# A two-layer hybrid backbone: the scan stage's decays in other buffers and first in a group, masks ahead of scaled keys, recurrence steps dealt out anew, gates loaded apart from rows

## The chip, the cores and the metric

The kernel runs on one core of one Trainium2 chip. The metric is the device time of one execution in microseconds; the figure given is the median of three runs. A profiled execution has a trace beside its own time.

## The reference, cut to what matters

Two layers are applied to 128 prompt rows and to 1024 sample rows. A layer projects its input, runs three token mixers on the same projection, projects their outputs together, and then applies a mixture of 16 experts. The change is in the token mixers: latent attention with 4 heads, gated linear attention (GLA) with 4 heads, and a gated delta net (GDN) with 8 heads. The last two run over chunks of 64 rows, in both directions. For the delta net a chunk needs the inverse of a unit lower triangular 64x64 matrix, and a state that goes from chunk to chunk:

```python
def gdn_chunked(q, k, v, beta, log_a, s0):
    ...
    g = jnp.cumsum(log_a, axis=2)
    ...
    m = jnp.einsum('bnihk,bnjhk->bnhij', k_beta, k) * jnp.exp(jnp.where(strict, diff, -jnp.inf))
    t_inv = lax.linalg.triangular_solve(m, eye, left_side=True, lower=True, unit_diagonal=True)
    u = jnp.einsum('bnhij,bnjhv->bnihv', t_inv, v * beta[..., None])
    w = jnp.einsum('bnhij,bnjhk->bnihk', t_inv, k_beta * jnp.exp(g)[..., None])
    qk = jnp.einsum('bnihk,bnjhk->bnhij', q, k) * jnp.exp(jnp.where(incl, diff, -jnp.inf))
    ...
    def step(s, inp):
        qc, kc, uc, wc, ac, dl = inp
        v_new = uc - jnp.einsum('bihk,bhkv->bihv', wc, s)
        o = jnp.einsum('bihk,bhkv->bihv', qc, s) + jnp.einsum('bhij,bjhv->bihv', ac, v_new)
        s = s * jnp.exp(dl)[..., None, None] + jnp.einsum('bihk,bihv->bhkv', kc, v_new)
        return s, o
```

## The kernel before

Each layer is a row of stages with barriers between them: `front` (projection), `scan` (the three mixers), `mixer_output`, `experts`. Each engine runs its own list of instructions in the order in which the code writes them; waits between engines are semaphores, counted from 1. The change touches `scan` alone.

`scan` (L939) goes through five groups of chunks (2, 4, 4, 4 and 4 chunks of 64 rows). Both directions are worked at once, one in partitions 0 to 63, the other in 64 to 127. A group g does this for the delta net:

- **Head.** `small` (cumulated gates, TensorE, then an exponential `eg` on ScalarE); `turn_keys` and `turn_queries` (TensorE transposes, evicted by ScalarE to `kq`); `decays` (two matmuls of 128x512 for each half of the group, then the exponential `dec` on ScalarE); on GpSimd `scaled_keys` (eight operations) and `mask` (four, on `dec`); `grams` (TensorE) and `masked_grams` (VectorE, grams times `dec`).
- **Solve.** `block_in` and `block_scaled` (VectorE) bring the diagonal 32x32 blocks to `NB` and `Tb`, in the buffer `late`; `substitute` (GpSimd, L1812) inverts them in 30 dependent steps of two operations, between the semaphores `sub_in` and `sub_done`.
- **Tail.** VectorE turns the six solved blocks back: `inverse_for_x` (two, signals `nb_v`), `inverse(1)` and `inverse(2)` (signal `ta_v`), `inverse(0)` and `inverse(3)` (`tb_v`). TensorE joins the blocks by `merge_x` (waits for `nb_v` and for `sg_v`), `merge_z` (waits for `ta_v`), then `weights` (waits for `tb_v`) and `values`; ScalarE evicts each.
- **Recurrence.** The chunks of the group k = g - 1 go through `read_state` (TensorE reads the state, VectorE corrects the values) and `write_state` (TensorE, then VectorE adds), in the course of group g.

The rest of a group is filled with GLA, two halves of two chunks each (`gla_gates`, `gla_turn`, `gla_scores`, `gla_values`, then `gla_state` twice; VectorE signals `sg_v` at the end of each `gla_state`), and with units of latent attention (`attend(i)`): odd units are scores, even ones turn the probabilities. Which step stands between which is written out by hand, for each engine by itself. SP issues the loads and stores in an order of its own, each wait holding up what follows. After group 4 the four chunks of its recurrence run in a last stretch with the last attention units, while SP loads for the next stage (`load_next`).

`dec` lies in the first half of `early`, whose second half holds the keys; E holds the gates of GLA, `gin` its rows.

## Time and profile before

| | us |
|---|---|
| median of 3 runs (4412.68 to 4423.40) | 4415.18 |
| profiled execution, its own time | 4419.75 |
| its span in the trace | 4418.0 |
| TensorE busy | 3911.6 (89%) |
| VectorE, ScalarE, GpSimd busy | 2156.0, 971.5, 1050.0 |
| scan of layer 0 (from its first matmul, 578.2, to the next stage's, 1141.3) | 563.1 |
| scan of layer 1 (2761.8 to 3322.3) | 560.5 |

A stage's length is not read from the shares of the whole span, which mix stages with different limits. Within the scan a group lasts from the end of one `values` to the end of the next. Busy time of TensorE is that of pipelined matmuls with modelled ends. Times in a timeline are counted from the span's start.

### The profile page before, as it was taken

What the parts mean: (1) busy time and instruction counts of PE and PEld (TensorE: products, weight loads), DVE (VectorE), ACT (ScalarE), POOL (GpSimd) and SP (SyncE); (2) the same over time, 40 slices, a digit from 0 to 9 for tenths busy, and PEclk for the clock granted to TensorE, in tenths of its full rate; (3) what the DMA queues carried; (4) which work ended last, traced back from release to release, by engine and by line L of the source; (5) the groups of instructions that cost most, each with busy time, mean ns of one, the idle gap of its engine ahead of it and who ended that gap; (6) DMA issues with size and microseconds to landing.
All of it is one profiled execution on the core that took longest, in us unless ns stands there. A gap on an engine that the chain in (4) does not pass through costs nothing. (4 is left out here: it accounts for less than half of the span.)

```text
span 4418.0 us, 80607 instructions
## 1 busy us (share of the span) xinstructions
PE 3911.6 (89%) x33780; PEld 3014.1 (68%) x33780; DVE 2156.0 (49%) x4908; ACT 971.5 (22%) x1962; POOL 1050.0 (24%) x1088
## 2 busy tenths in 40 slices
PE   4999968788897999999869998788888799999995
PEld 3444446676556999999844445466764489999995
DVE  3335045665555444544453440556656564445445
ACT  1233134444210000000033331444441100000001
POOL 0036035454220100001040360345432100011002
PEclk9999978888998999999989999888889899999998
DMA  7557353331526888888564651533325278888886
GB/s 262 175 186 247 137 132 68 89 72 52 195 86 209 292 279 284 282 290 293 176 229 162 220 206 56 126 78 81 73 84 204 81 236 285 287 293 280 287 289 208
DMA packets 557880, 836.20 MB, mean 189 GB/s; under 512 B 85865, under 2 KB 403369, under 8 KB 551373
## 3 DMA queue, kind: packets, MB, share of 16 engines
q1 hardware_dynamic: 474476, 720.51, 50.1%
q10 hardware_dynamic: 67840, 71.59, 4.9%
q0 software_dynamic: 15200, 38.94, 3.5%
q8 instruction: 267, 4.37, 0.4%
q14 instruction: 97, 0.79, 0.1%
HBM read 698.83 MB, written 132.10 MB: 188 GB/s over the span
## 5 line engine op out<-in xcount | busy, mean ns | idle before, releaser
L2611 PE MATMUL ffn_hb<-ffn_xT,ffn_w 128*128 128x144 f32 x8192 | 1048.5, 286 | 0.0
L2611 PEld LDWEIGHTS ffn_hb<-ffn_xT,ffn_w 128*128 128x128 f32 x8192 | 1019.6, 190 | 2.3 <-issue 1.0
L521 PE MATMUL front_acc<-late,front_xmT 128*128 128x512 f32 (+2 forms) x2304 | 879.7, 541 | 21.6 <-DVE front_xmT L782 18.3
L521 PEld LDWEIGHTS front_acc<-late,front_xmT 128*128 128x128 f32 x2304 | 437.3, 192 | 450.0 <-issue 419.0
L2619 PE MATMUL ffn_acc<-ffn_hT,ffn_w 128*128 128x144 f32 x4096 | 547.2, 287 | 0.0
L2619 PEld LDWEIGHTS ffn_acc<-ffn_hT,ffn_w 128*128 128x128 f32 x4096 | 518.5, 190 | 6.7 <-issue 6.7
L2654 ACT ACTIVATE ffn_en<-ffn_hb 128x144 f32<-128x144 f32 x256 | 74.2, 290 | 1447.0 <-PE ffn_hb L2611 1447.0
L2534 POOL DMA_INDIRECT ffn_xe<-scratch_xhat,ffn_g_idx x34 | 34.2, 1005 | 1478.0 <-DVEq L2719 1435.9
L2763 DVE TENSOR_TENSOR ffn_hT<-ffn_en,ffn_hb 128x144 f32<-128x144 f32 x256 | 77.8, 304 | 582.3 <-ACT ffn_en L2654 581.9
L2287 PE MATMUL mixer_acc<-late,mixer_oT 128*128 128x512 f32 x576 | 250.7, 593 | 3.0 <-ACT mixer_oT L2253 3.0
L2680 DVE TENSOR_SCALAR_CACHE_REDUCE ffn_junk<-ffn_row,ffn_pair 128x128 f32<-128x128 f32 (+2 forms) x324 | 245.3, 757 | 1.5
L1817 POOL TENSOR_TENSOR scan_prod<-late 128x30 f32<-128x30 f32 (+5 forms) x300 | 182.6, 609 | 221.7 <-POOLq L1834 199.0
L591 POOL TENSOR_TENSOR x_res<-x_res,early 128x1536 f32<-128x1536 f32 x18 | 72.4, 4022 | 554.1 <-DMA x_res<-scratch_proj 554.1
L2287 PEld LDWEIGHTS mixer_acc<-late,mixer_oT 128*128 128x128 f32 x576 | 108.0, 190 | 133.0 <-issue 129.1
L2679 DVE TENSOR_SCALAR_CACHE_REDUCE ffn_junk<-ffn_row,ffn_pair 128x128 f32<-128x128 f32 (+6 forms) x252 | 187.2, 743 | 4.4
L1370 PE MATMUL scan_ring<-x_res 128*128 128x512 f32 (+1 forms) x400 | 160.4, 534 | 12.2 <-ACT x_res L1674 4.5
L1819 POOL TENSOR_TENSOR late<-late,scan_prod 128x30 f32<-128x30 f32 (+5 forms) x300 | 162.6, 542 | 23.5
L1981 DVE TENSOR_REDUCE scan_top<-x_res 128x1 f32<-128x1152 f32 (+1 forms) x72 | 88.7, 1232 | 145.0 <-ACT x_res L1678 126.6
L1351 PE MATMUL scan_ring<-x_res 128*128 128x64 f32 x1168 | 138.9, 272 | 0.9 <-ACT x_res L1701 0.9
L1351 PEld LDWEIGHTS scan_ring<-x_res 128*128 128x128 f32 x1168 | 136.6, 192 | 1.4 <-ACT x_res L1701 1.2
L649 ACT ACTIVATE front_out<-front_acc 128x512 f32<-128x512 f32 (+1 forms) x90 | 49.7, 552 | 392.7 <-PE front_acc L521 392.7
L1370 PEld LDWEIGHTS scan_ring<-x_res 128*128 128x128 f32 x400 | 68.9, 199 | 97.2 <-ACT x_res L1674 48.2
(349 smaller groups left out, 5190.3 us busy)
## 6 DMA issues: line engine op xcount, KB each, us to landing
ffn_w<-in_w_e SPq DMA_DIRECT2D x384, 1024.0 KB, 9.4
x_res<-in_w_mod SPq DMA_DIRECT2D x40, 1024.0 KB, 5.7
x_res<-scratch_proj SPq DMA_DIRECT2D x36, 768.0 KB, 6.3
scratch_proj<-front_out ACTq DMA_DIRECT2D x90, 256.0 KB, 2.2
ffn_row<-scratch_affT SPq DMA_DIRECT2D x36, 576.0 KB, 4.5
late<-in_w_in ACTq DMA_DIRECT2D x8, 2048.0 KB, 12.1
early<-scratch_qkv SPq DMA_DIRECT2D x16, 1024.0 KB, 10.2
scratch_qkv<-x_res SPq DMA_DIRECT2D x18, 768.0 KB, 3.5
```

Of the source, the lines that this page charges most:

```text
L521: mm = pe.matmul(acc[:, U % 2, 0:size], xmT[:, k, t * P:(t + 1) * P], w[:, n % 2, k, 0:size], start=k == 0, stop=k == KD - 1)
L1351: mm = pe.matmul(b[:, P:P + VD], probT[:, k * P:(k + 1) * P], kv[:, h % 2, KEYS_W + (j0 + k) * VD:KEYS_W + (j0 + k + 1) * VD], start=k == ...
L1370: mm = pe.matmul(ring[:, i % 2, 0:size], qT[:, n % 4, :], kv[:, h % 2, k0 + at:k0 + at + size], start=True, stop=True)
L1817: pool.tensor_tensor(x, wide(Tb[:, 0:i, i], n), NB[:, i + 1:32, i].unsqueeze(1).to_broadcast([P, i, n]), ALU.mult).then_inc(own, step())
L1819: pool.tensor_tensor(Tb[:, 0:i, i + 1:32], Tb[:, 0:i, i + 1:32], x, ALU.add).then_inc(own, step())
L1981: dve.tensor_reduce(top[:, c], prob[:, n % 2, 0:w], AX.X, ALU.max).then_inc(own, step())
L2287: mm = pe.matmul(acc[:, t % 2, n * 512:(n + 1) * 512], oT[:, t % 2, k, :], wout[:, k, n * 512:(n + 1) * 512], start=k == 0, stop=k == KD - 1)
L2611: mm = pe.matmul(hb[:, b, i * CAP:(i + 1) * CAP], w[:, r, k, c:c + P], xT[:, s, k, :], start=k == 0, stop=k == KD - 1)
L2619: mm = pe.matmul(part(c), w2[:, r, j % WIDTH, c * P:(c + 1) * P], hT[:, b, :], start=j == 0 and c % PER_BANK == 0, stop=j == KF - 1, skip_ ...
L2679: dve.tensor_scalar(junk[:, 0:a - lo], row[:, lo:a], mine, 0.0, ALU.is_ge, ALU.add, accum_out=counts[:, t, 0:1]).then_inc(own, step())
L2680: dve.tensor_scalar(junk[:, a - lo:hi - lo], row[:, a:hi], mine, 0.0, ALU.is_gt, ALU.add, accum_out=counts[:, t, 1:2]).then_inc(own, step())
L2763: dve.tensor_tensor(hT[:, b, :], en[:, b], hb[:, b, CAP:2 * CAP], ALU.mult).then_inc(h_done, 1)
```

## The change

On every engine that takes part, the order within a group is written anew. The decays come first in a group from group 1 on, ahead of `small`, and are put where the solve's `NB` and `Tb` lie, so they wait for the group before to be turned. GpSimd masks before it scales keys. The recurrence of a group of four chunks had two chunks in the head and two in the filling; now the head has the last chunk's write of the group before it and chunk 0, the filling has chunks 1 and 2, and the last chunk's read stands between `merge_x` and `merge_z`. VectorE does both `gla_state` of the second half ahead of turning the blocks. TensorE gets two matmuls more, whose result nobody reads, between `sub_done` and `merge_x`. SP loads the gates (E) apart from the rows, and earlier. Lines of after are numbered by up to 32 more than those of before.

```diff
-dec = qk[:, :, 0:DQ]
+dec = B.late[:, 6 * 1024:8 * 1024].rearrange("p (m c) -> p m c", m=4)
...
+def load_gla_gates(h):
+    if h > 0:
+        sp.wait_ge(gT_p, h + 1)
+    for d in range(2):
+        sp.dma_start(E[half(d)], rows("gla_la", d, h * P, P, d * GQ, (d + 1) * GQ)).then_inc(ge_in, 16)
+
 def load_gla(h):
     if h > 0:
         sp.wait_ge(gV_p, h + 1)
     for d in range(2):
         sp.dma_start(gin[half(d)], rows("proj", d, h * P, P, C_GQ, C_GLR)).then_inc(gl_in, 16)
-        sp.dma_start(E[half(d)], rows("gla_la", d, h * P, P, d * GQ, (d + 1) * GQ)).then_inc(gl_in, 16)
...
     g = k + 1
     if g == GROUPS:
         load_next()
-    if k >= 0:
-        for m in range(2):
+    if g == GROUPS:
+        store_gdn(k - 1, 3)
+        for m in range(4):
             store_gdn(k, m)
-    if g < GROUPS:
-        if k >= 0 and g + 1 < GROUPS:
-            load_gates(g + 1)
-        if g + 1 < GROUPS:
-            load_qk(g + 1)
-        h = halves[g][0]
-        if h < 8:
-            load_gla(h + 1)
+        break
     if k >= 1:
-        for m in range(2, 4):
-            store_gdn(k, m)
-    if k >= 0 and k + 2 < GROUPS:
-        load_v(k + 2)
-    if k == 0:
+        store_gdn(k - 1, chunks[k - 1] - 1)
+        load_v(g)
+    if k == 1:
         sp.wait_ge(s_v, 3)
         for d in range(2):
             for a in range(2):
...
-    if g < GROUPS:
-        for h in halves[g]:
-            if h != halves[g][0] and h < 8:
-                load_gla(h + 1)
-            store_gla(h)
+    if k >= 0:
+        store_gdn(k, 0)
+        if g + 1 < GROUPS:
+            load_gates(g + 1)
+    if g + 1 < GROUPS:
+        load_qk(g + 1)
+    if halves[g][0] < 8:
+        load_gla_gates(halves[g][0] + 1)
+    if k >= 1:
+        store_gdn(k, 1)
+    if halves[g][0] < 8:
+        load_gla(halves[g][0] + 1)
+    if k >= 1:
+        store_gdn(k, 2)
+    for h in halves[g]:
+        if h != halves[g][0] and h < 8:
+            load_gla_gates(h + 1)
+            load_gla(h + 1)
+        store_gla(h)
...
 def turn_keys(g, i):
-    h = halves[g][i]
     if i == 0:
         pe.wait_ge(qk_in, 32 * g + 33)
-        if g:
-            pe.wait_ge(w_a, h + 1)
-    else:
-        pe.wait_ge(eg_a, g + 2)
+    if g:
+        pe.wait_ge(E_a, halves[g][i] + 2)
...
 def decays(g, i):
     pe.wait_ge(laM_l, g + 2)
-    pe.wait_ge(qT_a, halves[g][i] + 2)
+    if g == 0:
+        pe.wait_ge(qT_a, halves[g][i] + 2)
+    elif i == 0:
+        pe.wait_ge(w_a, halves[g][0] + 1)
+    else:
+        pe.wait_ge(eg_a, g + 2)
...
 def grams(g, m):
     s = g % 2
     if m < 2:
-        pe.wait_ge(E_a, halves[g][min(m, len(halves[g]) - 1)] + 2)
+        i = min(m, len(halves[g]) - 1)
+        pe.wait_ge(qT_a, halves[g][i] + 2)
+        pe.wait_ge(E_a, halves[g][i] + 2)
         pe.wait_ge(eg_a, g + 2)
...
     if g == GROUPS:
+        write_state(k - 1, 3)
         for m in range(4):
...
     else:
+        decays(g, 0)
+        small(g)
+        if k:
+            write_state(k - 1, chunks[k - 1] - 1)
+        decays(g, 1)
         for i in range(n):
             turn_keys(g, i)
         read_state(k, 0)
         for i in range(n):
             turn_queries(g, i)
-        write_state(k, 0)
-        for i in range(n):
-            decays(g, i)
-        read_state(k, 1)
         for m in range(2):
             grams(g, m)
-        write_state(k, 1)
+        write_state(k, 0)
         for m in range(2, chunks[g]):
             grams(g, m)
         attend(at)
...
         attend(at + 7)
         gla_state(g, h, 1)
         h = halves[g][1]
+        gla_gates(g, h)
         attend(at + 8)
-        gla_gates(g, h)
+        gla_turn(g, h)
         attend(at + 9)
-        gla_turn(g, h)
+        gla_scores(g, h)
         attend(at + 10)
-        gla_scores(g, h)
+        gla_values(g, h)
         attend(at + 11)
-        gla_values(g, h)
+        gla_state(g, h, 0)
         attend(at + 12)
-        gla_state(g, h, 0)
-        attend(at + 13)
         gla_state(g, h, 1)
-        attend(at + 14)
+        for i in range(13, 15):
+            attend(at + i)
     if g > 1:
         gla_gates(g, h)
         attend(at + 1)
...
         gla_turn(g, h)
-        write_state(k, 2)
+        write_state(k, 1)
         gla_scores(g, h)
         attend(at + 3)
         gla_values(g, h)
-        read_state(k, 3)
+        read_state(k, 2)
...
         attend(at + 9)
         gla_state(g, h, 0)
+        gla_state(g, h, 1)
         attend(at + 10)
-        gla_state(g, h, 1)
         attend(at + 11)
+    if g:
+        pe.wait_ge(o_v, first[k] + chunks[k])
+        pe.wait_ge(sub_done, g + 2)
+        for _ in range(2):
+            pe.matmul(pR[:, 0, :], ident, B.masks[:].rearrange("p k c -> p (k c)"), start=True, stop=True)
     for i in range(n):
         merge_x(g, i)
+    if g:
+        read_state(k, chunks[k] - 1)
     for i in range(n):
         merge_z(g, i)
...
 def decays(g, i):
     act.wait_ge(D_p, halves[g][i] + 2)
+    if g:
+        act.wait_ge(ta_v, 2 * g + 1)
+        act.wait_ge(tb_v, 2 * g + 1)
     act.activation(dec[:, 2 * i:2 * i + 2, :], pA[:, 2 * i:2 * i + 2, :], ACT.Exp).then_inc(E_a, 1)
...
+        decays(g, 0)
+        small(g)
+        decays(g, 1)
         for i in range(n):
             turned(g, i, 0, kT_p, kT_a)
         for i in range(n):
             turned(g, i, 1 + g % 2, qT_p, qT_a)
-        for i in range(n):
-            decays(g, i)
         attend(at)
     if g == 1:
...
 spread_gates(0)
 for g in range(GROUPS):
+    for i in range(len(halves[g])):
+        mask(g, i)
     for m in range(chunks[g]):
         scaled_keys(g, m)
-    for i in range(len(halves[g])):
-        mask(g, i)
...
     else:
+        if k:
+            write_state(k - 1, chunks[k - 1] - 1)
         read_state(k, 0)
-        write_state(k, 0)
-        read_state(k, 1)
         for m in range(2):
             masked_grams(g, m)
-        write_state(k, 1)
+        write_state(k, 0)
         for m in range(2, chunks[g]):
             masked_grams(g, m)
...
         attend(at + 9)
         gla_masked(h)
-        attend(at + 11)
     if g > 1:
+        read_state(k, 1)
...
         h = halves[g][1]
         gla_scaled(h)
         attend(at + 6)
         gla_masked(h)
         attend(at + 8)
     if g:
-        inverse_for_x(g)
         gla_state(h, 0)
-        inverse(1, ta_v)
-        if g > 1:
-            inverse(2, ta_v)
         gla_state(h, 1)
         if g == 1:
-            inverse(2, ta_v)
+            attend(at + 11)
+        inverse_for_x(g)
+        inverse(1, ta_v)
+        inverse(2, ta_v)
         inverse(0, tb_v)
         inverse(3, tb_v)
+        read_state(k, chunks[k] - 1)
         attend(at + (13 if g == 1 else 10))
     settle()
```

Two places of the order of instructions follow, of layer 0, first the end of group 3 on VectorE, from the last attention unit's last operation before the turning. `late` holds the solved blocks (before: L1891 is `inverse_for_x`, L1896 the `inverse` calls, L1938 to L1941 a `gla_state`, L1981 to L1993 an attention unit). Before:

```order
L1993 TENSOR_SCALAR x_res<-x_res,scan_rden 128x64
L1891 STREAM_TRANSPOSE late<-late 32x32x32 x2
L1938 TENSOR_TENSOR scan_og<-scan_og,scan_pA 128x2x2x64
L1939 TENSOR_TENSOR scan_SG<-scan_SG,scan_pA 128x256
L1941 TENSOR_TENSOR scan_SG<-scan_SG,scan_el 128x256
L1896 STREAM_TRANSPOSE late<-late 32x32x32 x2
L1938 TENSOR_TENSOR scan_og<-scan_og,scan_pA 128x2x2x64
L1939 TENSOR_TENSOR scan_SG<-scan_SG,scan_pA 128x256
L1941 TENSOR_TENSOR scan_SG<-scan_SG,scan_el 128x256
L1896 STREAM_TRANSPOSE late<-late 32x32x32 x2
```

And of the change, at the same place (L1921 and L1926 are the same calls, L1970 to L1973 a `gla_state`, L1932 to L1939 a `read_state`):

```order
L2025 TENSOR_SCALAR x_res<-x_res,scan_rden 128x64
L1970 TENSOR_TENSOR scan_og<-scan_og,scan_pA 128x2x2x64
L1971 TENSOR_TENSOR scan_SG<-scan_SG,scan_pA 128x256
L1973 TENSOR_TENSOR scan_SG<-scan_SG,scan_el 128x256
L1970 TENSOR_TENSOR scan_og<-scan_og,scan_pA 128x2x2x64
L1971 TENSOR_TENSOR scan_SG<-scan_SG,scan_pA 128x256
L1973 TENSOR_TENSOR scan_SG<-scan_SG,scan_el 128x256
L1921 STREAM_TRANSPOSE late<-late 32x32x32 x2
L1926 STREAM_TRANSPOSE late<-late 32x32x32 x4
L1932 TENSOR_TENSOR scan_sdec<-scan_S,scan_eg 128x512
L1935 TENSOR_TENSOR scan_v<-scan_v,scan_pR 128x2x4x64
L1939 TENSOR_TENSOR scan_od<-scan_pR,scan_eg 128x2x4x64
```

Both `gla_state` have moved ahead of the six turned blocks, which now stand in one row, with a `read_state` behind them.

The second place is the head of group 3 on TensorE, behind the last `values` (L1277) of group 2. Before (L1186 to L1189 are `small`, L1201 the keys, L1293 and L1297 a `read_state`, L1207 the queries, L1306 and L1314 a `write_state`, L1214 the decays, L1228 the grams):

```order
L1186 MATMUL scan_pA<-scan_la,masks_sb 128x32
L1187 MATMUL scan_pA<-scan_la,masks_sb 128x32
L1189 MATMUL scan_pA<-scan_RD,ones 64x32 x2
L1201 MATMUL scan_pA<-masks_sb,early 128x128 x16
L1293 MATMUL scan_pR<-scan_S,scan_nwT 64x64 x16
L1297 MATMUL scan_pR<-scan_S,scan_kq 64x64 x16
L1207 MATMUL scan_pA<-masks_sb,early 128x128 x16
L1306 MATMUL scan_pR<-scan_v,scan_kend 64x64 x16
L1314 MATMUL scan_pR<-scan_v,scan_A 64x64 x16
L1214 MATMUL scan_pA<-late,masks_sb 128x512 x4
L1293 MATMUL scan_pR<-scan_S,scan_nwT 64x64 x16
L1297 MATMUL scan_pR<-scan_S,scan_kq 64x64 x16
```

And of the change (L1228 are the decays now, L1198 to L1201 `small`, L1322 and L1330 a `write_state`, L1210 the keys, L1309 and L1313 a `read_state`, L1216 the queries, L1244 the grams):

```order
L1228 MATMUL scan_pA<-late,masks_sb 128x512 x2
L1198 MATMUL scan_pA<-scan_la,masks_sb 128x32
L1199 MATMUL scan_pA<-scan_la,masks_sb 128x32
L1201 MATMUL scan_pA<-scan_RD,ones 64x32 x2
L1322 MATMUL scan_pR<-scan_v,scan_kend 64x64 x16
L1330 MATMUL scan_pR<-scan_v,scan_A 64x64 x16
L1228 MATMUL scan_pA<-late,masks_sb 128x512 x2
L1210 MATMUL scan_pA<-masks_sb,early 128x128 x16
L1309 MATMUL scan_pR<-scan_S,scan_nwT 64x64 x16
L1313 MATMUL scan_pR<-scan_S,scan_kq 64x64 x16
L1216 MATMUL scan_pA<-masks_sb,early 128x128 x16
L1244 MATMUL scan_pA<-scan_kq 64x128 x32
```

The decays have moved to the front, half of them ahead of `small`; the head has one `read_state` less, and as many `write_state`, of which the first is that of the chunk before.

## Rows read from the trace of the kernel before

**Rows 1.** Stretches: length, busy us (instructions) of each engine, TensorE's granted clock, DMA share, GB/s.
```profile
697.80:797.40 99.60, 84.26 (x1450) 67.14 (x1448) 57.45 (x82) 46.83 (x91) 51.05 (x73) 0.86 0.39 86
...
898.00:997.80 99.80, 84.58 (x1690) 69.52 (x1690) 63.93 (x88) 44.66 (x83) 51.84 (x73) 0.88 0.36 77
...
sum 560.50, PE 444.87 PEld 353.93 DVE 326.59 ACT 237.70 POOL 245.97; mean PE 74.14 PEld 58.99 DVE 54.43 ACT 39.62 POOL 40.99
```

**Rows 2.** Waits of TensorE in groups 2 to 4: total us, times, longest.
```profile
PE scan_pA L1444 <- DVE scan_SG L1941: 16.6, 3, 8.5
...
PE scan_pA L1397 <- DMA scan_E<-scratch_gla_la: 0.9, 1, 0.9
```

**Rows 3.** Timeline of GpSimd in group 3: start, us, operation, idle before.
```profile
900.39 1.04 POOL L1807 TENSOR_TENSOR scan_kend<-early,scan_eg 128x512 f32<-128x512 f32 x1 [10.54 <-ACT scan_eg L1575]
...
909.51 5.02 POOL L1825 TENSOR_TENSOR early<-early,ids_sb 128x512 f32<-128x512 f32 x4 [1.07 <-ACT early L1586]
932.47 0.51 POOL L1817 TENSOR_TENSOR scan_prod<-late 128x30 f32<-128x30 f32 x1 [17.94 <-POOLq L1834]
...
971.95 0.26 POOL L1819 TENSOR_TENSOR late<-late,scan_prod 128x30 f32<-128x30 f32 x1
```

**Rows 4.** Timeline of VectorE in group 3.
```profile
917.83 0.68 DVE L1862 TENSOR_TENSOR scan_A<-scan_pA,early 128x512 f32<-128x512 f32 x1
...
932.10 0.20 DVE L1883 COPY late<-scan_betaT 128x32 f32<-128x32 f32 x1
...
972.32 3.90 DVE L1891 STREAM_TRANSPOSE late<-late 32x1024 f32<-32x1024 f32 x2 [3.52 <-POOLq L1837]
976.26 0.42 DVE L1938 TENSOR_TENSOR scan_og<-scan_og,scan_pA 128x256 f32<-128x256 f32 x1
...
977.50 4.15 DVE L1896 STREAM_TRANSPOSE late<-late 32x1024 f32<-32x1024 f32 x2
...
982.48 0.42 DVE L1941 TENSOR_TENSOR scan_SG<-scan_SG,scan_el 128x256 f32<-128x256 f32 x1
```

**Rows 5.** Timeline of TensorE at the end of group 3.
```profile
977.52 0.70 PE L1444 MATMUL scan_pA<-scan_SG,scan_gT 64*64 64x64 f32 x16 [3.45 <-DVE scan_SG L1941]
...
983.05 3.46 PE L1239 MATMUL scan_pA<-late 32*32 32x32 f32 x122 [2.62 <-DVE scan_SG L1941]
...
989.84 1.99 PE L1265 MATMUL scan_pA<-late 64*64 64x64 f32 x64
...
998.97 0.38 PE L1186 MATMUL scan_pA<-scan_la,masks_sb 128*128 128x32 f32 x2 [1.22 <-ACT scan_v L1622]
```

**Rows 6.** Timeline of TensorE in the head of group 3.
```profile
899.18 0.38 PE L1186 MATMUL scan_pA<-scan_la,masks_sb 128*128 128x32 f32 x2 [1.21 <-ACT scan_v L1622]
...
906.39 3.70 PE L1214 MATMUL scan_pA<-late,masks_sb 128*128 128x512 f32 x8
910.02 0.69 PE L1293 MATMUL scan_pR<-scan_S,scan_nwT 64*64 64x64 f32 x32
...
911.00 1.93 PE L1228 MATMUL scan_pA<-scan_kq 64*64 64x128 f32 x64
```

**Rows 7.** Timeline of group 1: VectorE, then TensorE.
```profile
773.60 4.05 DVE L1891 STREAM_TRANSPOSE late<-late 32x1024 f32<-32x1024 f32 x2
...
778.94 0.46 PE L1444 MATMUL scan_pA<-scan_SG,scan_gT 64*64 64x64 f32 x16
...
782.56 2.21 PE L1239 MATMUL scan_pA<-late 32*32 32x32 f32 x128 [1.55 <-DVE scan_SG L1941]
...
789.80 2.30 PE L1265 MATMUL scan_pA<-late 64*64 64x64 f32 x63
```

**Rows 8.** The last stretch: TensorE, SP's issue, and one of the stretches.
```profile
1097.73 0.69 PE L1293 MATMUL scan_pR<-scan_S,scan_nwT 64*64 64x64 f32 x32 [1.17 <-issue]
...
1098.94 2.00 SPq L1136 DMA_DIRECT2D late<-in_w_out  x4
...
1110.00:1115.00 5.00, 4.78 (x92) 4.41 (x91) 2.19 (x5) 1.58 (x5) 0.00 (x0) 1.00 0.71 273
```

36 lines of the change are left out of this document (20 added, 16 removed).

## The prediction

> **What bounds the kernel now.** I read the stretches first, because the change touches the scan stage alone. The table of stretches gives a row for each group, of which groups 1 and 3 of layer 0 stand here [rows 1]: each lasts about 100 us, and TensorE is busy for 84 to 85 of them, at a granted clock of 0.86 to 0.88. So TensorE is the busiest engine and yet idles 15 us in a group. The sum row of layer 1 says that the second scan takes 560.5 us, like the first, so what I find for one layer counts twice.
>
> Then I asked who makes TensorE wait, in the waits of groups 2 to 4. The largest wait is for VectorE's `scan_SG` [rows 2]: 16.6 us in three waits, the second `gla_state` of the second half of a group. To see what VectorE does then, I followed group 3 from engine to engine. TensorE ends the values of group 2 at 897.97 (899.18 less the wait of 1.21 us ahead of `small` [rows 6]; one group on it is 998.97 - 1.22 = 997.75 [rows 5]). VectorE finishes the masked grams at 917.83 + 0.68 = 918.5, and the start of the solve at 932.3 [rows 4]. GpSimd then substitutes, alone, from 932.47 to 972.2 [rows 3]: 39.7 us, which the change leaves as it is. VectorE turns the solved blocks from 972.32 on (two blocks, 3.90), does one `gla_state`, turns two more (4.15), does the other `gla_state`, whose last operation ends at 982.9 [rows 4], and only then does `merge_x` start, at 983.05 [rows 5]. `weights` follows at 989.84. The reader is to see a loop of about 99.8 us through GpSimd: head 34.3 (897.97 to 932.3), substitution 39.9, tail 17.6 (972.2 to 989.84), weights and values 7.9 (989.84 to 997.75). TensorE's attention work fills it, and is not what sets its length.
>
> **The tail.** `merge_x` waits for `nb_v` (first two blocks turned) and for `sg_v` (both `gla_state`). In the order of before the second comes last, because its operations on VectorE stand behind four of the six blocks to be turned. The change puts both `gla_state` of VectorE ahead of the turning, under the substitution, where VectorE has room. Then three pairs of transposes stand in a row: 3.9 + 4.15 + 4.15 = 12.2 us after the substitution `tb_v` is given (the third pair has the form of the second), and `weights` needs it. With 0.2 us for signals `weights` starts 12.4 us after the substitution instead of 17.6: **5.2 us** a group. This holds only if TensorE's own part is through by then: `merge_x` after 4 us, then `read_state` of the last chunk (the pair of rows 910.02 and 911.00 puts such a read at about 1.0 us), then `merge_z`. At full clock `merge_x` takes 2.21, at half 3.46 [rows 5, 7]. At full clock the sum 3.9 + 2.2 + 1.0 is under the 8.05 at which `ta_v` allows `merge_z`; `merge_z` and its eviction then end at about 12. So the tail is VectorE's.
>
> What may make TensorE late: its second `gla_state` now stands right behind the first, and waits for VectorE's three operations between them, 977.52 - 976.26 = 1.26 us [rows 4, 5], with the signals some 1.4. In group 3 that puts its last attention units some 1.4 us later while it had little to spare (it sat idle only 3.45 us before the `gla_state` at 977.52), and VectorE itself reaches the turning about 0.7 us after the substitution's end. I subtract **0.7 us** in group 3; groups 2 and 4 have the larger part of the 16.6 us of idle time and lose nothing. The two added matmuls of 128x512 (eight such took 3.70 as traced, so two take about 0.9 [rows 6]) run while the first blocks are turned; without that cover they cost those 0.9 us.
>
> **The head.** Gone from it are one `read_state` with its `write_state`; it gains the `write_state` of the chunk before. That is one read less, about 1.0 to 1.2 us. The first half of `decays` (half of 3.70) now stands ahead of `small`, where TensorE waited 1.22 us for the eviction of the values [rows 5, 6]; it needs only `w_a`, given earlier. Together 2.4 us. Something comes back: the decays used to stand between the transposes of the queries and the grams and so gave ScalarE time to evict; now the grams follow the transposes and wait for it, by 0.5 to 0.9 us. I take **1.9 us** for groups 2 to 4, between 0 (all of it lost in the eviction) and 2.4.
>
> Edits at nothing: masks ahead of the scaled keys on GpSimd. The first mask was at 909.51, behind eight scaled keys from 900.39 [rows 3]; the decays now come early and the masks with them, the scaled keys end some 8 us later. GpSimd then waits until 932.47 anyway, and `kend_l` and `Rk_l` are wanted in the tail; without that cover 8 us a group. The decays in `late` instead of `early` are written after `ta_v` and `tb_v` of the group before, long given. The gates of the gated linear attention (GLA) apart from its rows: the DMA wait ahead of the gates matmul goes, 0.9 us in groups 2 to 4 together [rows 2], and the next wait there is for `sg_v`. SP's queue holds `load_gates`, `load_qk` behind a `store_gdn`, and `load_gla` behind another; each has more than 10 us until it is wanted, and if not, the late group pays that part.
>
> **Group 1** has 15 units of attention and no room: TensorE itself ends the filling at 781.0, 1.55 us before `merge_x` at 782.56, and VectorE begins to turn at 773.60 [rows 7]. Here the change moves the second half's gates ahead of one unit, and all of its steps one unit earlier, and puts VectorE's unit 11 behind both `gla_state`. I follow it: the gates wait for `sg_v` with the unit that filled this time now behind them, and I count the 2 us that the head gives as used up there. The second `gla_state` on TensorE was at 778.94, behind a long unit; without that unit, and with the waits ahead of it, I put it at 775.5 to 776. VectorE's three operations end at 777.2, its unit 11 (a maximum over 1152 columns and small change, an estimate of 2 us) at 779.2, and turning starts there, 5.6 us later than now. `weights` then comes at 779.2 + 12.4 = 791.6 at best, against 789.80; and TensorE's unit 13 waits for the exponentials that wait for this maximum, some 3 us, at the risk of the clock. I take a **loss of 3.5 us**, between a gain of 2 (the head's gain kept) and a loss of 7.
>
> **The last stretch** gets a `write_state` ahead of its first read. It was at 1097.73, 1.17 us after the values [rows 8]; now the matmuls of a `write_state` (as many as a read's, with a wait between two parts: an estimate of 1.6 us) and VectorE's two additions (0.68 each, as 917.83 in [rows 4]) must be over: about 3.1 us after the values, a **loss of 2.0 us**. The added store of the delta-net rows goes to SP's queue behind the loads for the next stage, of which the last four are issued from 1098.94 to 1100.94 [rows 8], and the read of chunk 1, some 14 us after the values, wants its buffer. The loads keep the DMA engines busy at 0.71 still in the stretch from 1110 to 1115. If the store lands with the last of them, at 1112, VectorE waits 2 us, while TensorE works at an attention unit: nothing to 2 us. The Trainium skill's page DMA: Bandwidth & Descriptors, section Queues, rings and completion order, says that an engine takes a queue's descriptors in ring order; by that rule the upper end holds, and no row of before shows the landing.
>
> **The sum** for a layer: 3 x (5.2 + 1.9) - 0.7 - 3.5 - 2.0 = 15.1 us; for both, 30. The profiled execution took 4419.75, 4.6 above the median of 4415.18. So 4389.5 for an execution like it, and **4385** for a median.
>
> **Rivals.**
> - TensorE is late in the tails of groups 3 and 4. The new 1.4 us wait lowers the clock, the last two units and the merges run at half (3.46 instead of 2.21), and `weights` starts where it does now; only group 2 gains its 7.1, groups 3 and 4 together some 2.5. 9.6 - 5.5 = 4 a layer: 4407. For it: 2.62 us of waiting left `merge_x` at 3.46 for 122 matmuls. Against it: 1.55 us left it at 2.21 for 128 [rows 5, 7]. 15 in 100.
> - Group 1 keeps the pace and weights and values run at full clock in all groups: 3 x 7.1 + 2.5 - 2 = 22 a layer: 4371. 17 in 100.
> - `merge_x` is held by something else that I don't see, and nothing changes: 4415. 5 in 100.
> - Slower: that 1.4 us wait lowers the clock and it stays down through the values. Then weights start at about 989 as now and take 15.8 instead of 7.9 us: groups 3 and 4 lose 7 each, group 2 nothing, with 5.5 of group 1 and the last stretch 19 a layer: 4453. It decides where the clock doesn't come back before `weights`; in group 3 it was back there by 989.84 (64 matmuls in 1.99, then the values) even after two waits of 3.45 and 2.62. 5 in 100.
>
> My own case keeps 58 in 100, with its range 4374 to 4397. The range over the cases is 4366 to 4410: both ends of group 1 (11 us over two layers), of the head (0 to 2.4, six groups) and the first two rivals lie in it. A change under 0.3% (13 us) is about what a measurement of this kernel can't tell from none. Faster by more: 0.80 (my case, the second rival, a third of the first); the same: 0.14; slower: 0.06.
>
> **What would show it.** Right, if in groups 2 to 4 the first turned block follows the substitution at once, `weights` comes 12 to 13 us after it, and the groups last 92 to 94 us, with group 1 at 99 or more and the last stretch 2 us longer. Wrong, if TensorE's units still run when `nb_v` is given, if the head's masked grams end no sooner than 20 us after the values, or if group 1 loses more than 7 us.

## The result

The changed kernel takes 4428.69 us (median of 20 runs) against 4412.93 for the kernel before, measured beside it: a ratio of 1.0033 [1.0026, 1.0039], slower by some 15 us. The forecast was 4385 with a range of 4366 to 4410. The time lies outside it, on the slower side, to which the forecast gave 0.06.

The stretches of layer 0 in the changed kernel, groups 0 to 4 and the last stretch (length, then busy us and instructions of each engine, TensorE's granted clock, DMA share, GB/s), answer to [rows 1]:

```profile
577.50:702.25 124.75, 85.16 (x767) 58.50 (x767) 65.02 (x135) 46.87 (x99) 43.83 (x67) 0.79 0.47 112
702.25:808.85 106.60, 85.77 (x1391) 67.58 (x1389) 58.53 (x79) 46.37 (x91) 50.87 (x73) 0.87 0.28 65
808.85:903.35 94.50, 81.60 (x1669) 65.05 (x1667) 62.14 (x88) 41.47 (x79) 51.86 (x73) 0.93 0.43 96
903.35:1001.60 98.25, 85.18 (x1695) 67.55 (x1695) 64.67 (x88) 44.62 (x83) 51.88 (x73) 0.93 0.35 78
1001.60:1095.95 94.35, 78.52 (x1674) 63.32 (x1672) 61.08 (x84) 41.46 (x79) 48.15 (x72) 0.95 0.21 48
1095.95:1147.20 51.25, 36.90 (x719) 30.60 (x715) 19.97 (x37) 16.41 (x35) 0.01 (x1) 0.89 0.41 139
```

Read in the same way, both kernels and both layers stand against the forecast like this, in us a layer:

| | before, layers 0 / 1 | after | forecast | measured |
|---|---|---|---|---|
| group 0 | 119.6 / 117.3 | 124.7 / 124.7 | 0 | +5.1 / +7.4 |
| group 1 | 99.6 / 99.1 | 106.6 / 105.4 | +3.5 | +6.9 / +6.3 |
| groups 2 to 4 | 299.1 / 299.6 | 287.1 / 287.5 | -20.6 | -12.0 / -12.1 |
| last stretch | 44.8 / 44.7 | 51.3 / 49.8 | +2.0 | +6.5 / +5.1 |
| scan | 563.1 / 560.6 | 569.7 / 567.3 | -15.1 | +6.6 / +6.7 |

The two scans together are 13.3 us longer. The profiled executions differ by 5.6 us alone (4425.33 against 4419.75), because the stages that the change does not touch were 7.7 us shorter in the second one; so the parts are read from the stretches, not from the difference of two profiles.

The gain is there where it was expected, at 0.6 of its size, and three other places lose more than it. TensorE's waits for the second `gla_state` in groups 2 to 4 (total us, times, longest) are no longer the largest, which is now that of `gla_turn` (L1423); [rows 2] had 16.6 us:

```profile
PE scan_pA L1423 <- DVE scan_Ei L1956: 12.5, 4, 4.6
...
PE scan_pA L1461 <- DVE scan_SG L1973: 4.0, 3, 1.3
```

Each place has its rows.

**Group 0.** GpSimd, VectorE and TensorE in the changed kernel (L1855 mask, L1837 and L1838 scaled keys, L1996 the rotation of queries in VectorE's `first_latents`, L1359 TensorE's transposes of those queries):

```profile
602.35 2.57 POOL L1855 TENSOR_TENSOR late<-late,ids_sb 128x512 f32<-128x512 f32 x2 [25.37 <-ACT late L1615]
...
604.88 1.04 POOL L1837 TENSOR_TENSOR scan_kend<-early,scan_eg 128x512 f32<-128x512 f32 x1
604.92 4.08 DVE L1996 SCALAR_TENSOR_TENSOR x_res<-x_res,qss,rope_sb 128x64 f32<-128x64 f32 x4
...
607.88 1.03 POOL L1838 TENSOR_TENSOR late<-early,scan_eg 128x512 f32<-128x512 f32 x1
...
610.12 0.84 PE L1359 MATMUL scan_ring<-masks_sb,x_res 128*128 128x128 f32 x4 [2.88 <-ACT x_res L1667]
```

And before, the first scaled keys and the same four operations of VectorE:

```profile
584.15 1.04 POOL L1807 TENSOR_TENSOR scan_kend<-early,scan_eg 128x512 f32<-128x512 f32 x1 [6.47 <-DMA early<-scratch_qkv]
...
605.35 0.86 DVE L1964 SCALAR_TENSOR_TENSOR x_res<-x_res,qss,rope_sb 128x64 f32<-128x64 f32 x4
```

The four scaled keys ran at 584 to 588, while VectorE had nothing to do. Behind the masks they run at 604.88 to 608.9, beside four operations of VectorE that now take 4.08 us instead of 0.86, one for each operation of GpSimd. TensorE waits 2.88 us for their product, which reaches it through an eviction on ScalarE (L1667).

**Group 1.** The end of GpSimd's substitution, then VectorE (L2013 the maximum of unit 11, L1921 the first blocks turned):

```profile
773.25 0.27 POOL L1849 TENSOR_TENSOR late<-late,scan_prod 128x30 f32<-128x30 f32 x1
...
781.72 1.35 DVE L2013 TENSOR_REDUCE scan_top<-x_res 128x1 f32<-128x1152 f32 x1
...
783.61 4.01 DVE L1921 STREAM_TRANSPOSE late<-late 32x1024 f32<-32x1024 f32 x2
```

And TensorE (L1386 scores and L1367 values of unit 13, L1585 the two added matmuls, L1255 `merge_x`, L1281 `weights`):

```profile
785.18 0.79 PE L1386 MATMUL scan_ring<-x_res 128*128 128x128 f32 x2 [2.91 <-ACT x_res L1703]
785.76 3.94 PE L1367 MATMUL scan_ring<-x_res 128*128 128x64 f32 x18
...
791.43 1.88 PE L1585 MATMUL scan_pR<-masks_sb 128*128 128x512 f32 x4
793.24 2.21 PE L1255 MATMUL scan_pA<-late 32*32 32x32 f32 x128
...
801.07 1.63 PE L1281 MATMUL scan_pA<-late 64*64 64x64 f32 x64
```

The substitution ends at 773.5 and turning begins at 783.61, 10.1 us later; [rows 7] had it at once. On TensorE unit 13 waits 2.91 us for exponentials, whose maximum VectorE took at 781.72, and its values then run at half clock (granted 0.50; 3.94 us, where 2.12 is their time at full). `weights` comes 27.5 us after the substitution, 16.7 before.

**Group 3**, TensorE at its end (L1461 the second `gla_state`, L1386 the scores behind it):

```profile
975.15 0.46 PE L1461 MATMUL scan_pA<-scan_SG,scan_gT 64*64 64x64 f32 x16 [1.33 <-DVE scan_SG L1973]
975.54 3.90 PE L1386 MATMUL scan_ring<-x_res 128*128 128x512 f32 x6
...
983.12 1.89 PE L1585 MATMUL scan_pR<-masks_sb 128*128 128x512 f32 x4
984.94 2.21 PE L1255 MATMUL scan_pA<-late 32*32 32x32 f32 x128
...
991.81 0.68 PE L1281 MATMUL scan_pA<-late 64*64 64x64 f32 x27 [0.29 <-ACT late L1643]
```

The substitution ended at 976.4 and VectorE turned blocks from 976.98 to 989.5, as forecast. But the unit behind the 1.33 us wait ran at half clock (granted 0.55; 3.90 us for six scores instead of 2.30), the two added matmuls came behind it, and `merge_x` began 4 us after `nb_v`. `weights` starts 15.4 us after the substitution: less than the 17.6 of [rows 5], more than the 12.4 forecast.

**The last stretch**: SP's queue (L1142 the last loads for the next stage, L1096 the store of chunk 3 of group 3), the first read on TensorE (L1309), VectorE's read of chunk 1 and TensorE behind it:

```profile
1099.02 0.69 PE L1309 MATMUL scan_pR<-scan_S,scan_nwT 64*64 64x64 f32 x32 [1.49 <-DVE scan_od L1949]
...
1099.25 2.62 SPq L1142 DMA_DIRECT2D late<-in_w_out  x4
1101.91 0.60 SPq L1096 DMA_DIRECT2D scratch_scan_f<-scan_od  x1
...
1116.47 0.69 DVE L1939 TENSOR_TENSOR scan_od<-scan_pR,scan_eg 128x512 f32<-128x512 f32 x1 [6.42 <-DMA scratch_scan_b<-scan_od]
...
1117.22 1.13 PE L1322 MATMUL scan_pR<-scan_v,scan_kend 64*64 64x64 f32 x32 [3.73 <-DVE scan_od L1939]
1118.13 1.92 PE L1330 MATMUL scan_pR<-scan_v,scan_A 64*64 64x64 f32 x32
```

The store is issued behind the loads, and VectorE, which waits 6.42 us for its buffer, goes on 14.6 us after the issue. TensorE waits 3.73 us and then works at half clock (granted 0.50; 1.13 and 1.92 us, 0.69 and 1.10 at full).

### The profile page after: what moved, and what is told of

Read it like the earlier page. It is cut to its first block and busy times, and to the rows that moved or that the text cites. A ratio compares the mean times of both kernels' runs of the same rounds, so it can differ in the third digit from the quotient of the medians.

```text
span 4423.5 us, 80727 instructions
## 1 busy us (share of the span) xinstructions
PE 3918.6 (89%) x33812; PEld 3007.1 (68%) x33812; DVE 2146.6 (49%) x4908; ACT 970.0 (22%) x1962; POOL 1048.2 (24%) x1088
## 5 line engine op out<-in xcount | busy, mean ns | idle before, releaser
L521 PE MATMUL front_acc<-late,front_xmT 128*128 128x512 f32 (+2 forms) x2304 | 879.7, 541 | 19.4 <-DVE front_xmT L782 17.6
L591 POOL TENSOR_TENSOR x_res<-x_res,early 128x1536 f32<-128x1536 f32 x18 | 75.8, 4208 | 552.6 <-DMA x_res<-scratch_proj 552.6
L1386 PE MATMUL scan_ring<-x_res 128*128 128x512 f32 (+1 forms) x400 | 162.8, 538 | 20.4 <-ACT x_res L1703 12.5
L2013 DVE TENSOR_REDUCE scan_top<-x_res 128x1 f32<-128x1152 f32 (+1 forms) x72 | 88.6, 1231 | 139.6 <-ACT x_res L1707 121.4
L1367 PE MATMUL scan_ring<-x_res 128*128 128x64 f32 x1168 | 142.5, 277 | 0.9 <-ACT x_res L1730 0.9
L1386 PEld LDWEIGHTS scan_ring<-x_res 128*128 128x128 f32 x400 | 69.6, 201 | 107.4 <-ACT x_res L1703 56.3
L1367 PEld LDWEIGHTS scan_ring<-x_res 128*128 128x128 f32 x1168 | 140.0, 196 | 1.4 <-ACT x_res L1730 1.2
L1703 ACT ACTIVATE x_res<-scan_ring 128x512 f32<-128x512 f32 (+1 forms) x200 | 94.0, 481 | 197.5 <-PE scan_ring L1367 115.9
```

Of the source, the lines that this page charges most:

```text
L521: mm = pe.matmul(acc[:, U % 2, 0:size], xmT[:, k, t * P:(t + 1) * P], w[:, n % 2, k, 0:size], start=k == 0, stop=k == KD - 1)
L1367: mm = pe.matmul(b[:, P:P + VD], probT[:, k * P:(k + 1) * P], kv[:, h % 2, KEYS_W + (j0 + k) * VD:KEYS_W + (j0 + k + 1) * VD], start=k == ...
L1386: mm = pe.matmul(ring[:, i % 2, 0:size], qT[:, n % 4, :], kv[:, h % 2, k0 + at:k0 + at + size], start=True, stop=True)
L1703: ins = act.activation(prob[:, n % 2, at:at + size], ring[:, i % 2, 0:size], ACT.Copy)
L2013: dve.tensor_reduce(top[:, c], prob[:, n % 2, 0:w], AX.X, ALU.max).then_inc(own, step())
```

## The experiments

Ratios are to the kernel before, run beside it on the same chip, with a 95% interval; a ratio of 0.0010 is 4.4 us. Not all runs were made on one chip, so they are compared with each other by their ratios. Lengths of groups are those of single traces. The change alone is 1.0033 [1.0026, 1.0039]. The first five undo one thing each.

**Scaled keys first in group 0.**

```diff
 for g in range(GROUPS):
+    if g == 0:
+        for m in range(chunks[g]):
+            scaled_keys(g, m)
     for i in range(len(halves[g])):
         mask(g, i)
-    for m in range(chunks[g]):
-        scaled_keys(g, m)
+    if g:
+        for m in range(chunks[g]):
+            scaled_keys(g, m)
```

> Group 0 alone gets GpSimd's old order back: scaled keys, then masks. Theory (VectorE's four rope operations, L1996, take 4.08 us instead of 0.86 because GpSimd's scaled keys run beside them, and TensorE waits 2.88 us for what they make): the four go back to about 0.9 us, the scaled keys to some 20 us earlier, group 0 of layer 0 from 124.8 to 120 or 121 us, and the median falls by 8 us, to about 4421. Rival (the 5 us of group 0 come from the new order of loads on SP, or from the clock at the start): group 0 stays at 124 to 125 and the median at about 4429.

1.0016 [1.0008, 1.0025]. Group 0 takes 119.8 and 118.5 us in the two layers (group 1 1.4 and 2.2 us more than in the change), and VectorE's four operations are back at 0.86, from this timeline:

```profile
604.13 0.86 DVE L2000 SCALAR_TENSOR_TENSOR x_res<-x_res,qss,rope_sb 128x64 f32<-128x64 f32 x4
```

The loads on SP stayed as in the change, so the loss of group 0 is the order on GpSimd, and its size here is 5 to 6 us a layer.

**The maximum of unit 11 ahead of the gla_state (group 1).**

```diff
+    if g == 1:
+        attend(at + 11)
     gla_state(h, 0)
     gla_state(h, 1)
-    if g == 1:
-        attend(at + 11)
     inverse_for_x(g)
```

> Group 1 alone: VectorE does unit 11 ahead of both gla_state again; TensorE's order stays that of the change. Theory (in group 1 TensorE is late because unit 13 waits for exponentials that wait for the maximum of unit 11 behind both gla_state): the wait of 2.91 us ahead of the scores of unit 13 and its half clock go, merge_x comes at about 788.5 instead of 793.2, weights at about 796 instead of 801 (times of layer 0), group 1 takes about 102 us instead of 106.6, and the median falls by 9 us, to about 4420. Rival (the wait only moves: VectorE is still at the maximum when the first gla_state comes, so the second one on TensorE and the turning of blocks come later by as much): group 1 falls by 1 us or less, median 4427.

1.0027 [1.0017, 1.0038]; group 1 takes 106.3 and 104.6 us, against 106.6 and 105.4. The rival held: the wait only moved. TensorE now stands ahead of its second `gla_state`, and the unit behind it runs at half clock:

```profile
782.68 0.71 PE L1461 MATMUL scan_pA<-scan_SG,scan_gT 64*64 64x64 f32 x16 [1.51 <-DVE scan_SG L1973]
783.31 4.21 PE L1386 MATMUL scan_ring<-x_res 128*128 128x512 f32 x6
```

So it is not the place of the maximum alone. Both `gla_state` of group 1 come after the substitution's end, and turning behind them is late in any case.

**The store ahead of the loads (last stretch).**

```diff
     if g == GROUPS:
-        load_next()
         store_gdn(k - 1, 3)
+        load_next()
```

> SP alone: the store of chunk 3 of group 3 is issued ahead of the loads for the next stage instead of behind them. Theory (the store lands only after those loads, and VectorE's read of chunk 1 waits 6.4 us for its buffer): that wait goes, with TensorE's 3.7 us behind it and the half clock of the matmuls after it, the last stretch of layer 0 falls from 51.3 to 46 or 47 us, and the median by 10 us, to about 4419; what stays over the 44.7 us of before is the added write of the state, about 2 us. Rival (the store takes its time anyway, or the loads, now some 4 us later, are waited for at the end of the stage): 50 us or more, median 4427 to 4429.

1.0014 [1.0004, 1.0025]. The last stretch, in the table of stretches:

```profile
1098.93:1145.36 46.43, 34.57 (x719) 28.51 (x709) 19.97 (x37) 16.36 (x35) 0.04 (x1) 0.93 0.47 154
```

VectorE's wait of 6.42 us is gone:

```profile
1112.76 0.68 DVE L1938 TENSOR_TENSOR scan_od<-scan_pR,scan_eg 128x512 f32<-128x512 f32 x1
```

The stretch takes 46.4 us in both layers, so the place in the queue cost 3.3 to 4.9 us. The 1.7 that remain over 44.7 fit the added write of the state, which no run leaves out by itself.

**Without the two matmuls at the merges.**

```diff
         pe.wait_ge(sub_done, g + 2)
-        for _ in range(2):
-            pe.matmul(pR[:, 0, :], ident, B.masks[:]...)
```

> The two added matmuls whose result nobody reads are left out; the waits ahead of them stay. Theory (TensorE is late at the merges of groups 1 to 3, and these 1.8 us lie on its path there; in group 4 VectorE is late, and nothing changes): merge_x 1.7 us earlier, groups 1, 2 and 3 shorter by 1.6, 1.1 and 1.6 us, the median lower by 9 us, at about 4420, with merge_x still at 2.2 us. Rival (they keep the clock up): merge_x and merge_z at half clock in one or more groups (3.5 us for merge_x), groups 1 to 3 as long as now or up to 3 us longer, median 4429 to 4445.

1.0020 [1.0011, 1.0028]. `merge_x` stays at 2.2 us in groups 1 and 3, and `merge_x` of group 2 takes 3.62 in both layers, in layer 0 behind a wait of 3.03 us:

```profile
891.58 3.62 PE L1255 MATMUL scan_pA<-late 32*32 32x32 f32 x128 [3.03 <-DVE late L1919]
```

Groups 2 to 4 add up to 283.6 and 284.8 us, 568.4 together; in the six traces that have these groups as in the change it is 573.7 to 577.4. `merge_x` starts 0.2 to 0.6 us after `nb_v` in groups 2 to 4 of both layers, where those six traces have 0.0 to 3.9, on average 2.0. Group 1 stays at 106.5 and 105.5, so the matmuls are no part of its loss. Both expectations are half right: a merge falls to half clock, and still the matmuls cost more than they give, some 6 us.

**The order of before in group 1**, on TensorE, ScalarE and VectorE:

```diff
 # TensorE and ScalarE: gates and later steps of the second half behind a unit more (left out here)
 ...
 # VectorE, group 1
-    gla_state(h, 0)
-    gla_state(h, 1)
-    attend(at + 11)
-    inverse_for_x(g)
-    inverse(1, ta_v)
+    attend(at + 11)
+    inverse_for_x(g)
+    gla_state(h, 0)
+    inverse(1, ta_v)
+    gla_state(h, 1)
     inverse(2, ta_v)
```

> Group 1 alone gets the order of before back, on TensorE, ScalarE and VectorE: gates of the second half behind a unit more, the first two blocks turned ahead of the gla_state, which stand between the transposes again. Theory (in group 1 both gla_state come only some 5 to 9 us after the end of the substitution, so turning behind them makes VectorE late, and with it the last units and merges): turning starts within 1 us of the substitution's end instead of 10 us after it, group 1 takes 100 to 102 us instead of 105 to 107, the median falls by 11 us, to 0.1% over the kernel before. Rival (group 1 is late for the head, or for the added read and matmuls between and ahead of the merges): 104 us or more, the median falls by less than 5.

0.9994 [0.9984, 1.0004]: about 17 us back, more than expected. Group 1 takes 97.6 and 95.8 us. VectorE's first turned blocks and TensorE's `weights`:

```profile
774.80 4.09 DVE L1921 STREAM_TRANSPOSE late<-late 32x1024 f32<-32x1024 f32 x2
...
792.69 1.99 PE L1281 MATMUL scan_pA<-late 64*64 64x64 f32 x64
```

Turning starts 0.1 us after the substitution (774.42 + 0.27), and `weights` 18.0 us after it. So group 1 takes no longer than in the two runs below that leave it as it was (97.0 to 98.8 us). With the new head the substitution starts 33 us after the values instead of 37, but against those two runs the end of the group does not show it.

**Three mends together** (scaled keys, store, group 1).

> Three mends together: scaled keys ahead of masks in group 0, the order of before in group 1, the store of chunk 3 of group 3 ahead of the loads for the next stage. If the three losses are separate, the gains add: 5 to 6 us of group 0, 4 of the last stretch and 5.5 of group 1 a layer, 30 us for both, so a time 0.3 to 0.4% under the kernel before, about 4396. Rival (a gain in one group is lost to the clock or to a wait in the next): within 0.1% of the kernel before, 4406 to 4415.

0.9961 [0.9948, 0.9974], 4393.06 us. The losses add: from 1.0033 to 0.9961 is 0.72% or 32 us, and 30 were expected.

**The three mends, with the two matmuls between the gla_state, and without them.**

```diff
     gla_state(g, h, 0)
+    two matmuls 128x512, result not read   (in the first of the two runs alone)
     gla_state(g, h, 1)
     attend(at + 10)
...
-    the two matmuls ahead of merge_x       (in both)
```

> The three mends, and the two matmuls that nobody reads moved from the merges to the place between the two gla_state of the second half (in group 1 left out), where TensorE waits 1.33 us. Theory (this wait costs the clock in some groups, and at the merges the matmuls lie on TensorE's path): groups 2 and 3 fall from 95 and 98 us to 93 to 94, group 4 stays at 94, and the time is 10 to 14 us under that of the three mends alone, some 0.65% under the kernel before. Rival (only their place at the merges costs): 5 to 7 us under the three mends. Third (they hold the clock up for the merges): no gain or a loss, merge_x at 3.5 us.

> The three mends, and the two matmuls that nobody reads left out altogether. It parts two readings of what they cost at the merges and gave between the two gla_state (0.61% under the kernel before there, 0.39% with them at the merges). Theory (both count: off the merges 6 us, in the wait of 1.33 us another 4): 0.52% under the kernel before, about 4387, with some of the units behind the second gla_state at half clock (3.5 us and more instead of 2.3). Rival (only their place at the merges cost): 0.6% under it, like the filled one, about 4383.

0.9939 [0.9925, 0.9954], 4383.33 us, and 0.9946 [0.9932, 0.9960], 4385.29 us. They can't be told apart. Against the three mends alone both are lower, by some 10 and 7 us, though both intervals overlap with theirs; with the 6 us of the run above (1.0020 against 1.0033), and `merge_x` again at 0.2 to 0.6 us after `nb_v` in every group from 2 to 4, this speaks for the place at the merges as what costs. In the first of them TensorE has no wait between the two `gla_state` (L1460):

```profile
961.73 0.46 PE L1460 MATMUL scan_pA<-scan_SG,scan_gT 64*64 64x64 f32 x16
962.12 1.98 PE L1579 MATMUL scan_pR<-masks_sb 128*128 128x512 f32 x4
964.03 0.46 PE L1460 MATMUL scan_pA<-scan_SG,scan_gT 64*64 64x64 f32 x16
964.43 2.30 PE L1385 MATMUL scan_ring<-x_res 128*128 128x512 f32 x6
```

In the second it has the wait, and the unit behind it runs at full clock all the same, as do all six such units of this run:

```profile
962.16 0.46 PE L1460 MATMUL scan_pA<-scan_SG,scan_gT 64*64 64x64 f32 x16 [1.33 <-DVE scan_SG L1974]
962.56 2.30 PE L1385 MATMUL scan_ring<-x_res 128*128 128x512 f32 x6
```

**The kernel before, with the tail alone.**

```diff
 # TensorE, groups 2 to 4
     gla_state(g, h, 0)
-    attend(at + 10)
     gla_state(g, h, 1)
+    attend(at + 10)
     attend(at + 11)
 # VectorE, groups 2 to 4
+    gla_state(h, 0)
+    gla_state(h, 1)
     inverse_for_x(g)
-    gla_state(h, 0)
     inverse(1, ta_v)
     inverse(2, ta_v)
-    gla_state(h, 1)
```

> The kernel before with one part of the change alone: in groups 2 to 4 VectorE does both gla_state ahead of turning the six blocks, and TensorE the second one right behind the first, ahead of unit 10. Everything else is that of before. Theory (the tail as predicted): weights 12.4 us after the substitution instead of 17.6, groups 2 to 4 shorter by 5 us each, less 0.7 in group 3, 30 us for both layers, about 4381. Rival (TensorE is late behind its new wait, at half clock in some groups): groups 2 and 4 gain 4 to 5, group 3 nothing to 2, 16 to 24 us in all, 4387 to 4395. Third (the head was where the gain came from): under 8 us.

0.9936 [0.9923, 0.9948], 4384.23 us: by the ratio 28 us under the kernel before. No run has a lower ratio, though 0.9939 above can't be told from it. Group 3 of layer 0, VectorE (L1891 and L1896 the turned blocks) and TensorE (L1239 `merge_x`, L1265 `weights`):

```profile
968.15 4.04 DVE L1891 STREAM_TRANSPOSE late<-late 32x1024 f32<-32x1024 f32 x2
...
972.23 8.31 DVE L1896 STREAM_TRANSPOSE late<-late 32x1024 f32<-32x1024 f32 x4
...
972.78 2.21 PE L1239 MATMUL scan_pA<-late 32*32 32x32 f32 x128
...
980.79 1.98 PE L1265 MATMUL scan_pA<-late 64*64 64x64 f32 x64 [1.91 <-DVE late L1896]
```

`merge_x` follows `nb_v` (972.2) within 0.6 us, `weights` waits for VectorE alone, 13.2 us after the substitution (967.56). Groups 2 to 4 have 12.7 to 13.6, on average 13.1 where before had 17.7: 4.6 us a group.

**The tail alone, with the two matmuls between the gla_state.**

> The kernel before with the tail alone, and two matmuls that nobody reads between the two gla_state of the second half in groups 2 to 4. With the tail alone two of six units behind the second gla_state ran at half clock (3.56 and 3.58 us instead of 2.30). Theory (the filled wait keeps the clock): six of six at 2.3 us, but the second gla_state and the turning of blocks some 0.5 us later, so no more than 3 us in all: 0.64 to 0.7% under the kernel before. Rival (the clock falls there whatever stands in the wait): one or more units at half, and a loss of 2 to 4 us against the tail alone.

0.9946 [0.9932, 0.9959]: no gain, though all six units behind ran at 2.30.

**The tail, and the decays first in a group**, without and with those two matmuls. With the decays come their place in the solve's buffer and the masks ahead of the scaled keys, but for group 0; the recurrence stays as it was:

```diff
 # TensorE, groups 1 to 4, from small to grams
+    decays(g, 0)
     small(g)
+    decays(g, 1)
     turn_keys, read_state(k, 0), turn_queries
     write_state(k, 0)
-    decays(g, i) for each half
     read_state(k, 1)
```

> The kernel before with two parts of the change: the tail alone, and the decays first in a group in the solve's buffers with masks ahead of scaled keys (in group 0 the old order); the recurrence stays as it was dealt before. Theory (the head's gain is the wait ahead of small, 1.2 us, which the decays now cover, less what the grams wait for the transposes): masked grams end 1.0 us sooner after the values, four groups and two layers make 8 us: 0.8% under the kernel before, 4375. Rival (the head gained by the read that left it, not by the decays): masked grams at 20.5 us as before, time as with the tail alone, 0.64% under. Third (GpSimd's scaled keys now run beside VectorE's work in the head and stretch it): masked grams later, a loss.

> As the run before (tail alone, decays first), with the two matmuls between the two gla_state. If both gains are real and separate, 0 to 3 us under that run, 0.8 to 0.9% under the kernel before, 4371 to 4375; if the matmuls only push the turning back, 2 to 4 us over it.

0.9965 [0.9951, 0.9979] and 0.9977 [0.9966, 0.9988]: slower than the tail alone by 0.29%, some 13 us, and more; groups 2 to 4 of both layers take 582.0 and 582.5 us, 573.6 with the tail alone. The masked grams of groups 2 to 4 end at 22.1 to 22.5 us after the values, not at 19.6. The third case expected masked grams that come later, and a loss, but for a cause that the trace doesn't show: beside GpSimd's scaled keys (L1816) VectorE's masked grams (L1874) take the 0.68 us that they take elsewhere.

```profile
908.27 1.04 POOL L1816 TENSOR_TENSOR scan_kend<-early,scan_eg 128x512 f32<-128x512 f32 x1
...
908.91 0.68 DVE L1874 TENSOR_TENSOR late<-scan_pA,late 128x512 f32<-128x512 f32 x1
```

The cause is on TensorE. Its second half of `decays` and second read in the head of group 3:

```profile
896.22 1.96 PE L1216 MATMUL scan_pA<-late,masks_sb 128*128 128x512 f32 x4 [0.74 <-ACT scan_eg L1580]
...
906.48 0.69 PE L1297 MATMUL scan_pR<-scan_S,scan_nwT 64*64 64x64 f32 x32 [1.56 <-DVE scan_od L1931]
```

The decays had stood between a write and the next read, 3.70 us in [rows 6], and hid VectorE's additions. Moved ahead, they leave the read to wait 1.56 us, and the second half waits 0.74 for `eg`.

## Why the prediction was wrong

No single step did it. A layer's scan came out 21.7 us longer than forecast: 8.6 and 8.5 us of this (layers 0 and 1) lie in groups 2 to 4, 5.1 and 7.4 in group 0, 4.5 and 3.1 in the last stretch, 3.4 and 2.8 in group 1. In groups 2 to 4 the tail gave 1.8 us a group less than its term and the head 1.2. One step failed by its reason, the masks put at nothing; the others are terms that were mis-sized. One of the forecast's own signs of being wrong came too: in group 3 `nb_v` was given at 981.0, and TensorE's last unit and the two matmuls behind it kept `merge_x` back until 984.94.

- **The tail, 5.2 us a group: right in kind.** Alone it gives 4.6. In the change it gave 3.4 (`weights` at 12.7 to 17.6 us after the substitution, on average 14.35 against 17.75), since TensorE was late at `merge_x`: behind the two matmuls, and in some groups at half clock behind the wait of 1.33 us.
- **The two matmuls, "about 0.9", hidden: mis-sized twice.** I took eight rows of [rows 6] for eight matmuls of the code. A matmul of 128x512 stands as two there; the two are x4 and 1.88 us. And the cover was missing where TensorE came late. Off the merges, 6 to 10 us come back, by ratios whose intervals overlap.
- **The 1.4 us wait: size right, consequence left to a rival.** I took 0.7 us in group 3 and the clock's fall as a rival of 15 in 100. In the traces of ten kernels with this wait (1.33 to 1.56 us) 20 of 60 units behind it ran at half clock, in no fixed group; with the wait filled, none of 18. That the filling does it is not shown: in the two kernels with the wait and without any added matmul at the merges none of 12 ran at half clock either, while it was 16 of 36 in the six that have the matmuls there, and 4 of 12 in the two that add the tail to the kernel before, without added matmuls. What decides it stays open. What it is worth in time stays under what the runs can tell (0.9939 against 0.9946, and 0.9946 against 0.9936).
- **The head, 1.9 us: mis-sized, and credited to the wrong part.** Masked grams end on average 0.7 us sooner (19.1 to 20.8 us after the values; 20.5 to 20.7 before). The decays ahead of `small` lose 1.5 us when the recurrence keeps its second read, because they were its cover; so the gain comes with the recurrence dealt out anew, which takes that read out of the head. I counted the wait that they hide and not the one that they bared.
- **GpSimd's masks first, at nothing: the step that failed outright.** I named GpSimd's own idle time as cover and asked who waits for the keys, not who works beside them. In group 0 this cost 5 to 6 us a layer. The Trainium skill's page SBUF — State Buffer, section Who interferes with whom, says that a VectorE instruction with two inputs in SBUF contends with a GpSimd instruction that reads SBUF, and that one holds the shared ports while the other waits. The trace agrees: four operations in 4.08 us beside four of 1.04, and 0.86 without them.
- **Group 1, a loss of 3.5: 6.9 and 6.3.** Its turning began 5.6 us later in the group, as I had worked out (81.4 us after the values against 75.8). What I took for a risk, the exponentials that wait for the maximum "at the risk of the clock", came: 2.91 us of waiting and 1.8 of half clock, and `weights` followed the start of turning by 17.5 us, not 12.4. (The two matmuls stand in the same rows, but without them the group took as long.) The larger fault is of kind: I let the tail's order stand there as a small loss, where [rows 7] show that the premise (both `gla_state` done under the substitution) doesn't hold. With the old order on all three engines the loss is gone.
- **The last stretch, 2.0: 6.5 and 5.1.** The write was right as far as the rows tell: the first read starts 3.1 us after the values, as forecast, and 1.7 us remain when the store is mended. The store, "nothing to 2 us", cost 3.3 to 4.9: I put its landing at the end of the loads at 1112, and VectorE went on at 1116.47. The forecast cited the Trainium skill's page DMA: Bandwidth & Descriptors, section Queues, rings and completion order, which says that each DMA engine takes a queue's descriptors in ring order. The runs agree: issued ahead of the loads, the store no longer makes VectorE wait 6.42 us. The landing that I drew from that order was too early.
- **The rival on the slower side** (the clock stays down through the values) was not what happened: weights to the end of the values took 8.2 us on average in groups 2 to 4, as before. What did make it slower was in the text as a small term, or at nothing.

The parts that come apart are these: tail alone -28 us; group 0, group 1 and the store some +32 together; the two matmuls +6. They add up to +10 of the 15 measured. What the rest does (the recurrence dealt out anew, the read between the merges, gates apart) was not tried by itself; mended and without the matmuls the change is at 0.9946, the tail alone at 0.9936, so together it gives nothing that these ratios could show. The two traces hint at two things that cancel: groups 2 to 4 of both layers take 566.9 us in the mended one against 573.6 with the tail alone, the last stretches 92.9 against 89.2. The same code spread over 3.8 us in the six traces above, so this is no more than a hint.

## What to carry to other kernels

Before moving work on an engine that "waits anyway", look at what the other engines do at the new time, not only at who needs its result: GpSimd's free time was VectorE's busy time. An operation that stands in a chain may be cover for the wait behind it; count the wait that its move bares, as well as the one that it hides. And when one order is applied to all groups, check its premise in each: here the tail's order gave all of the gain in groups 2 to 4, and the order of the change in group 1 took more than half of that back (17 us of 28).

## What the runs showed of the hardware

In group 0 four operations of VectorE with both inputs in SBUF took 1.08 us each, one beside each of GpSimd's operations of 1.04, where the kernel before has 0.86 us for all four: each took as long as the operation of GpSimd beside it. It is not the only place. The product of `read_state` with both inputs in SBUF (0.68 us alone) took 1.07 to 1.21 us seven times in the two scans of the kernel before, and 1.05 to 3.81 seven times in the changed kernel, each time beside GpSimd. Here it meets GpSimd's `spread_gates`:

```profile
987.60 3.66 POOL L1828 TENSOR_TENSOR late<-scan_la,ids_sb 128x2048 f32<-128x2048 f32 x1 [11.22 <-PE scan_pA L1255]
...
989.52 2.29 DVE L1932 TENSOR_TENSOR scan_sdec<-scan_S,scan_eg 128x512 f32<-128x512 f32 x1
```

It ends 0.55 us after GpSimd does (991.81 and 991.26). Masked grams, which take one input from PSUM (TensorE's output buffer), kept their 0.68 us beside scaled keys.

The wait of 1.33 to 1.56 us on TensorE, at the same place of the program, was followed by full clock in 40 cases and by half in 20. Its length does not tell them apart: waits of 1.33 us stand on both sides.
